# Wider first transfer of x, one copy of the norm weights and six narrower-operand warm-ups in a two-layer decoder kernel

## The reference

```python
def hybrid_layer(x, attn_norm, w_in, moba_out_norm, dil_out_norm, w_out, mlp_norm, w_up, w_down, cos, sin):
    h = rms_norm(x, attn_norm)            # x * rsqrt(mean(x*x) + eps) * gain
    qa, ka, va, qd, kd, vd = split(h @ w_in)              # 1024 -> 3072, 8 + 8 heads of 64
    out_a = rms_norm(causal_attention(rope(qa), rope(ka), va), moba_out_norm)
    out_d = rms_norm(dilated_attention(rope(qd), rope(kd), vd), dil_out_norm)
    x = x + concatenate([out_a, out_d]) @ w_out
    h = rms_norm(x, mlp_norm)
    return x + square(relu(h @ w_up)) @ w_down            # 1024 -> 4096 -> 1024
# two layers, then rms_norm(x, final_norm)
```

## Time and profile before

| | |
|---|---|
| median of 3 runs | 591.47 us (591.19 to 591.62) |
| the profiled execution | 591.49 us, span 589.8 us |
| TensorE busy | 581.0 us, 99% of the span |
| VectorE, ScalarE, GpSimd busy | 405.3, 314.2, 65.7 us |
| moved by DMA | 104.18 MB, mean 177 GB/s |

### The profile page before, as it was taken

One profiled execution on the slowest core, in us unless ns is written; L12 is line 12 of the kernel. 1 busy time (PEld: TensorE's weight loads), 2 busy tenths in 40 slices (PEclk: granted clock), 3 DMA queues, 4 the chain that ended last, 5 costly groups with the idle time before them and its releaser, 6 DMA issues.

```text
span 589.8 us, 9170 instructions
## 1 busy us (share of the span) xinstructions
PE 581.0 (99%) x3293; PEld 489.2 (83%) x3293; DVE 405.3 (69%) x652; ACT 314.2 (53%) x525; POOL 65.7 (11%) x67
## 2 busy tenths in 40 slices
PE   8999999999999999999999999999999999999995
PEld 6888877888888888888888888778888888888884
DVE  5897887597656656556379879768876656656634
ACT  5856867375445345344285765774645345345322
POOL 0242330210000000000005225112000000000001
PEclk9999999999999999999999999999999999999998
DMA  8955243258664564564264643442885564564301
GB/s 298 379 206 190 107 142 126 91 173 305 197 236 158 178 239 151 188 238 143 71 205 155 215 141 144 144 142 72 254 260 199 165 235 169 169 236 164 107 0 71
DMA packets 58859, 104.18 MB, mean 177 GB/s; under 512 B 1824, under 2 KB 35152, under 8 KB 58832
## 3 DMA queue, kind: packets, MB, share of 16 engines
q1 hardware_dynamic: 58256, 102.92, 51.8%
q10 hardware_dynamic: 576, 0.92, 0.5%
HBM read 102.79 MB, written 1.05 MB: 176 GB/s over the span
## 4 chain that ended last, share of the span: by engine, by line
PE 96%; DMA 1%; DVE 1%; ACT 1%; issue 0%; SPq 0%; POOLq 0%; POOL 0%; DVEq 0%
PE psum L1204 20%; PE psum L986 15%; PE psum L988 15%; PE psum L987 15%; PE psum L1207 10%; PE psum L1007 9%; PE psum L1012 4%; PE psum L1141 2%; PE psum L1160 2%; DMA raw<-in_w_in 1%; PE psum L1177 1%; PE psum L993 1%; PE psum L1180 1%; ACT xt L531 0%; DVE x L735 0%
## 5 line engine op out<-in xcount | busy, mean ns | idle before, releaser
L701 DVE TENSOR_TENSOR w_lo<-raw,w_hi 128x1024 fp32r<-128x1024 f32 x188 | 228.2, 1247 | 52.1 <-ACT w_hi L525 52.0
L525 ACT CAST w_hi<-raw 128x1024 fp32r<-128x1024 f32 x188 | 186.5, 1047 | 3.5 <-DMA raw<-in_w_in 2.8
L1204 PE MATMUL psum<-xt,w_hi 128*128 128x512 f32 x512 | 160.8, 395 | 0.0
L986 PE MATMUL psum<-w_hi,ot_hi 128*128 128x512 f32 x320 | 126.9, 397 | 0.0
L988 PE MATMUL psum<-w_hi,ot_lo 128*128 128x512 f32 x320 | 124.9, 390 | 0.0
L987 PE MATMUL psum<-w_lo,ot_hi 128*128 128x512 f32 x320 | 124.8, 390 | 0.0
L1207 PEld LDWEIGHTS psum<-xt,w_lo 128*128 128x128 f32 x512 | 96.2, 188 | 22.3
L1207 PE MATMUL psum<-xt,w_lo 128*128 128x256 f32 x512 | 100.7, 278 | 0.0
L1204 PEld LDWEIGHTS psum<-xt,w_hi 128*128 128x128 f32 x512 | 80.2, 189 | 2.3
L645 ACT COPY up_cross<-psum 128x512 f32<-128x512 f32 x32 | 18.8, 587 | 118.8 <-PE psum L1207 118.8
L879 DVE TENSOR_TENSOR up_cross<-psum,up_cross 128x512 f32<-128x512 f32 x32 | 22.1, 690 | 74.1 <-ACT up_cross L645 74.1
(11 more groups left out here) (98 smaller groups left out, 537.6 us busy)
## 6 DMA issues: line engine op xcount, KB each, us to landing
raw<-in_w_up SPq DMA_DIRECT2D x32, 1024.0 KB, 5.6
raw<-in_w_down SPq DMA_DIRECT2D x32, 1024.0 KB, 6.6
raw<-in_w_in SPq DMA_DIRECT2D x21, 1024.0 KB, 5.9
raw<-in_w_out SPq DMA_DIRECT2D x8, 1024.0 KB, 4.8
raw<-in_w_in SPq DMA_DIRECT2D x3, 512.0 KB, 8.2
raw<-in_w_in SPq DMA_DIRECT2D x4, 256.0 KB, 4.7
out<-x SPq DMA_DIRECT2D x3, 256.0 KB, 2.4
raw<-in_w_in ACTq DMA_DIRECT2D x2, 256.0 KB, 4.7
```

The source lines that it names most:

```text
L525: act.copy(dst, src).then_inc(hi_done, 1)
L701: dve.tensor_tensor(lo_t, src, hi_t, ALU.subtract).then_inc(split_done, 1)
L986: pe.matmul(out, s_hi, m_hi, start=first, stop=False)
L1204: pe.matmul(up_banks[b][:, f, :], w_hi[:, slot, cols[f]], xt[:, k, :, :].rearrange("p a b -> p (a b)"), start=k == 0, stop=False)
```

## The change

Four edits in one. SP's and ScalarE's first transfers of x carry columns 0 to 511 instead of 0 to 255, and SP's separate transfer of columns 256 to 511 is gone, with its semaphore. `gains` holds both layers' 48 columns and is written by one copy; `gains_all`, `keep_gains` and the copy at each layer's end are gone, and every use picks its layer's column. The ones of the warm-ups are 128 columns, repeated four times by the operand's access pattern, and there are six warm-ups at the start instead of seven.

```diff
-        gains_all = sb("gains_all", [n_gains + layer_gains])
-        gains = sb("gains", [layer_gains])
+        gains = sb("gains", [n_gains])
...
+        def layer_gain(l, n):
+            return gains[:, l * layer_gains + n:l * layer_gains + n + 1]
...
-            sp.dma_start(x[:, 0, 0:SEQ], x_v[:, 0, 0:SEQ]).then_inc(x_loaded[0], 16)
+            sp.dma_start(x[:, 0, 0:BANK], x_v[:, 0, 0:BANK]).then_inc(x_loaded[0], 16)
             sp.dma_start(gain_rows[:, :], gain_rows_d).then_inc(gains_loaded, 16)
-            sp.dma_start(x[:, :, SEQ:BANK], x_v[:, :, SEQ:BANK]).then_inc(x_loaded[1], 16)
...
-            act.dma_start(x[:, 1, 0:SEQ], x_v[:, 1, 0:SEQ]).then_inc(x_loaded[0], 16)
+            act.dma_start(x[:, 1, 0:BANK], x_v[:, 1, 0:BANK]).then_inc(x_loaded[0], 16)
...
                 act.wait_ge(turned, l * TRS + n + 1)
-                if n == TR_X:
-                    act.wait_ge(gains_done, l + 1)
-                act.activation(dst, tile, ACT.Copy, scale=gains[:, gain:gain + 1]).then_inc(turned_hi, 1)
+                act.activation(dst, tile, ACT.Copy, scale=layer_gain(l, gain)).then_inc(turned_hi, 1)
...
                     act.wait_ge(weights_used, UNITS_HELD)
+                    act.wait_ge(gains_kept, 1)
                     x_to_hi(l, 0)
...
-            dve.memset(squares[:, 1, 0:BANK], 1.0).then_inc(ones_set, 1)
+            dve.memset(squares[:, 1, 0:P], 1.0).then_inc(ones_set, 1)
 
             dve.wait_ge(gains_turned, 1)
-            dve.tensor_copy(gains[:, :], banks[7][:, 0:layer_gains]).then_inc(gains_done, 1)
-
-            def keep_gains():
-                dve.tensor_copy(gains_all[:, 0:n_gains], banks[7][:, 0:n_gains])
-                dve.tensor_copy(gains_all[:, n_gains:n_gains + layer_gains], banks[7][:, 0:layer_gains])\
-                    .then_inc(gains_kept, 1)
+            dve.tensor_copy(gains[:, :], banks[7][:, 0:n_gains]).then_inc(gains_kept, 1)
...
-                dve.wait_ge(gains_kept, 1)
-                dve.wait_ge(turned_lo, (l + 1) * TRS)
-                dve.tensor_copy(gains[:, :], gains_all[:, bass.ds((l + 1) * layer_gains, layer_gains)])\
-                    .then_inc(gains_done, 1)
...
-                    pe.matmul(banks[6][:, :], squares[:, 1, 0:P], squares[:, 1, 0:BANK], start=True, stop=True)
-
-            warm_up(7)
+                    pe.matmul(banks[6].rearrange("p (n q) -> p n q", q=P), squares[:, 1, 0:P],
+                              squares[:, 1:2, 0:P].broadcast_to([P, BANK // P, P]), start=True, stop=True)
+
+            warm_up(6)
...
                     if s == 1 and l == 0:
-                        pe.wait_ge(x_loaded[1], 16)
                         turn_x(x_banks, range(2, 3))
```

More of the change, by code:

```diff
@@ L191, in hybrid_kernel @@
         up_banks = [psum[:, 4:6, :], psum[:, 6:8, :]]
-        x_loaded = [sem(f"x_loaded{n}") for n in range(3)]
+        x_loaded = [sem(f"x_loaded{n}") for n in range(2)]
         masks_loaded = sem("masks_loaded")
@@ L225, in hybrid_kernel @@
         rope_scaled = sem("rope_scaled")
-        gains_done = sem("gains_done")
         rope_terms = sem("rope_terms")
@@ L327, in o_tile, with o_gain @@
             return o_bank[:, p % 2 * SEQ:(p % 2 + 1) * SEQ]
-        def o_gain(p):
-            column = p + (2 * KT + SET_PAIRS if p < SET_PAIRS else 2 * KT - SET_PAIRS)
-            return gains[:, column:column + 1]
+        def layer_gain(l, n):
+            return gains[:, l * layer_gains + n:l * layer_gains + n + 1]
+        def o_gain(l, p):
+            return layer_gain(l, p + (2 * KT + SET_PAIRS if p < SET_PAIRS else 2 * KT - SET_PAIRS))
         def visit(l, c):
@@ L370, in _ @@
                                      at(in_v[:, :, k:k + 1, cols], l)).then_inc((tile_loaded[2], raw_ready[0])[k - 2], 16)
-                    sp.dma_start(x[:, :, BANK:D_MODEL], x_v[:, :, BANK:D_MODEL]).then_inc(x_loaded[2], 16)
+                    sp.dma_start(x[:, :, BANK:D_MODEL], x_v[:, :, BANK:D_MODEL]).then_inc(x_loaded[1], 16)
                     for half in range(2):
@@ L539, in o_to_hi @@
             def o_to_hi(l, p):
-                act.activation(ot_hi[:, p, :], o_tile(p), ACT.Copy, scale=o_gain(p)).then_inc(o_hi_done, 1)
+                act.activation(ot_hi[:, p, :], o_tile(p), ACT.Copy, scale=o_gain(l, p)).then_inc(o_hi_done, 1)
             def square_sums(l, n):
@@ L705, in turned_to_lo @@
                 dve.wait_ge(turned_hi, l * TRS + left + 1)
-                dve.scalar_tensor_tensor(out=lo_t, in0=tile, scalar=gains[:, gain:gain + 1],
+                dve.scalar_tensor_tensor(out=lo_t, in0=tile, scalar=layer_gain(l, gain),
                                          in1=hi_t.bitcast(F32), op0=ALU.mult, op1=ALU.subtract)\
@@ L714, in o_to_lo @@
                 dve.wait_ge(o_hi_done, l * PAIRS + LAST_PAIR[p] + 1)
-                dve.scalar_tensor_tensor(out=ot_lo[:, p, :], in0=o_tile(p), scalar=o_gain(p),
+                dve.scalar_tensor_tensor(out=ot_lo[:, p, :], in0=o_tile(p), scalar=o_gain(l, p),
                                          in1=ot_hi[:, p, :].bitcast(F32), op0=ALU.mult, op1=ALU.subtract)\
@@ L798, in _ @@
                     dve.tensor_copy(tile_apart(w_hi, 0), as_loaded(raw[:, 0, 0:BANK])).then_inc(first_tile_hi, 1)
-                    dve.wait_ge(gains_done, 1)
+                    dve.wait_ge(gains_kept, 1)
                     for k in range(4):
@@ L802, in _ @@
                         x_lo(k)
-                        if k == 1:
-                            keep_gains()
                     tile_to_lo(4)
@@ L1260, in _ @@
                     if s == (3 if l == 0 else 2):
-                        pe.wait_ge(x_loaded[2], 16)
+                        pe.wait_ge(x_loaded[1], 16)
                         pe.wait_ge(x_updated, l * 4 + 4)
```

## The result

The changed kernel took 593.05 us (median of 16 runs, 592.05 to 593.98), the kernel before 591.41 us (median of 16, 590.94 to 591.71): 1.64 us more, a ratio of 1.0026, 95% interval [1.0019, 1.0033]. The forecast was 591.6, and the range ended at 592.8. The mechanism that decided is that of rival B, which had 0.14. The profiled execution took 592.73 us, span 591.0, 1.24 us more than that of before: one of the shorter of the 16. One execution of the kernel before, taken beside the experiments, was slowed as a whole (644.48 us at a granted clock of 0.85) and is counted nowhere.

A forecast was written before the change was run, and what follows sets the result against it. TensorE, busy 99% of the span, was taken to bound the kernel. 0.50 us late at the first k, less 0.09 and 0.24 filled, gave +0.17 us, so 591.65, rounded to 591.6; range 590.9 to 592.8.

The forecast's parts named there:

- rival B: At the start, the 0.7 us hole after the warm-ups keeps TensorE at 1.2 GHz: +1.4 us, 593.0; chance 0.14.
- What bounds it: Whole kernel: TensorE, busy 581.0 us, 99% of the span, sets the time; other engines have room.
- (4), the warm-ups: Start: smaller memset, six warm-ups from 1.47 to near 4.0, TensorE then idle 0.7 us, at no cost by itself.
- the profile's sign: What the profile would show under rival B: groups of four matmuls spaced 0.85 us behind 6.3.
- the transfers' term: Start: TensorE 0.50 us late at the first k, less the 0.09 and 0.24 it fills: +0.17 us.
- (1), the transfers: Start: wider transfers of x delay tile k = 0 from 5.2 to 6.1 and TensorE's second group by 0.50 us.
- The upper bound of 8.1: Latest landing of tile k = 1, cast by 8.75, making TensorE 0.25 us later still.
- The slack: TensorE before 17 us: holes of 0.09 and 0.24 us, 0.33 in all, that a late start can use up.
- (2), what comes back: Tiles k = 4 and 5: fewer packets and a shorter SP queue give back 0.06 to 0.77 us; landing not later.
- (3), the norm weights: Norm weights' copies: one 0.02 us longer, hidden; the dropped copies, 0.4 and 0.18 us, gain nothing.

The follow-up runs named there:

- b_warm3: The kernel before with three warm-ups instead of seven, its transfers and copies unchanged: 592.62 us, ratio 1.0017.
- a_warm7: The changed kernel with seven warm-ups at the start instead of six: 592.72 us, ratio 1.0020.
- b_wide: The kernel before with the wide first transfers of x alone, seven warm-ups and old copies kept: 591.92 us, ratio 1.0016.
- a_rowsfirst8: The changed kernel with eight warm-ups and SP issuing the norm weights before x: 592.16 us, ratio 1.0020.
- b_gains: The kernel before with the one copy of the norm weights alone, everything else as before: 591.41 us, ratio 1.0000.
- a_late6: The changed kernel with its six warm-ups begun later, at 2.11 instead of 1.30 us, behind an extra VectorE memset: 592.91 us, ratio 1.0026.
- a_warm8: The changed kernel with eight warm-ups at the start instead of six: 591.83 us, ratio 1.0010.
- a_xapart8: The changed kernel with the old narrow transfers of x and eight warm-ups instead of six: 591.36 us, ratio 1.0000.

## Why the prediction was wrong

**What bounds it.** Right. TensorE's stream sets the time: 1.30 us of lateness at the seventh k became 1.24 at the end.

**(4), the warm-ups.** This is the step that failed: "By itself that costs nothing, as transfers bound the start". The hole was forecast at 0.7 us and measured 1.08, as the memset took 0.17 instead of 0.25 us and started a little earlier (the warm-ups start at 1.30, not 1.47), and the norm weights landed at 5.0 and not 4.8 and were taken at 5.13. What stood in the place of "nothing" is the clock: 13 of 16 executions of the changed kernel are above 592.5, and with two warm-ups more, which lift it early in 10 of 11, 1.1 us of the median go.

Rival B had this mechanism, with the price (+1.1 us for a k at the lower level, 593.0 in sum) and the profile's sign (0.85 us between groups, which is what 7.79 and 8.64 show). It assumed that the first k and half of the second would be low, +1.4 us; it was just the first k in the profiled execution, 1.19 us of the second k's lateness. That B's sum of 593.0 meets the median of 593.05 is in part luck: its clock term was too large by about 0.2 to 0.3 us, and the transfers' term of 0.17 too small by 0.4. The transfers' miss alone would have left the time near 592.0, inside the range; the clock's took it out.

B's chance was the mistake. I held against it that the hole is short and transposes stand after it. b_warm3 and a_warm7 (a hole of 0.76 us, 7 of 11 late) show that neither protects. In the profiled executions the link is complete: the three with a rise past 9 us took 592.31, 592.71 and 592.73, and the ten others of the table, all with a rise by 7.2, took 591.07 to 591.92.

**(1), the transfers.** The direction was right, the size too small: +0.17 forecast, +0.56 measured in b_wide's lower group. Its terms: the transposes were priced at 0 to 0.1 late and were 0.41 late in b_wide, because the norm weights' landing was put at 4.7 to 4.9 and came at 5.1 there. The tile k = 0 was put at 6.1, and came near 5.7 in the changed kernel and 5.9 in b_wide, the lower bound or just above; the second group was 0.31 late in b_wide (7.19 against 6.88) where 0.50 was forecast. The tile k = 1 was put at 7.35 to 7.4 and called hidden; it came at 7.8, and it is the wait that TensorE meets. The upper bound of 8.1 for it was in the text, with its price of 0.25 us. So lateness moved to the tile behind the one that I watched. The slack was there: the changed kernel was 1.65 us late at the second k and 1.30 at the seventh, and the seventh k's weights were no longer waited for.

The direction holds beyond one pair of profiles. With the wide transfer the norm weights landed at 5.0 to 5.2, the tile k = 0 at 5.7 to 5.9 and the tile k = 1 at 7.5 to 7.9 (the six that keep the order of the issues, and a_rowsfirst8 for the tiles); with the old ones at 4.1 to 4.4, 4.9 to 5.6 and 6.6 to 7.4, in seven profiles each.

**(2), what comes back.** The direction was right: the tiles k = 4 and 5 landed at 10.9 instead of 11.8, 0.9 us earlier (forecast 0.06 to 0.77). Part of this is chance, for the seven profiles with the old transfers have this landing anywhere from 11.0 to 11.8, and the seven with the wide one from 10.9 to 11.2. SP issued these tiles 0.21 us earlier (3.42 instead of 3.63) and not at least 0.42, as the text had it for every later tile. Nothing waited for them any more, so all this only let the slack be used.

**(3), the norm weights.** Right: b_gains is at 1.0000.

**The clock's page.** By the Trainium skill (TensorE: Matmul & The Clock Gate, Part 4) transposes don't count as activity the way matmuls do. The runs show that they run at either level, 0.11 us apart at the upper and 0.21 at the lower; whether they count for the rise is not shown, since every kernel here has the same ones.

**What stays open.** How much work and how small a hole it takes, and what makes the executions of one kernel fall in two groups. The runs point to both influences (a_late6 against b_wide: 9 and 3 of 11 late, with one warm-up less, begun later, and the same hole; a_rowsfirst8 against a_warm8: 5 and 1 of 11, the same warm-ups with the hole grown), and to no rule. Both pairs ran on different chips, and the second difference is small for eleven executions. Part of it is not in the kernel at all: before and b_gains do the same work up to 5.3 us and rose near 5.4 and near 6.7. In the five profiled kernels without a hole, and the two whose hole opened only after the rise, the rise came 3.1 to 5.9 us after the start of the first warm-up (b_wide, a_xapart8). If a hole only matters in executions whose clock has not risen by then, two groups follow; no late execution was profiled beside an early one of the same kernel, so this is argued and not shown. One execution of each kernel was profiled, so the late groups of a_warm7, b_wide and a_rowsfirst8 are put to the clock by their distance, some 1.0 to 1.3 us between the medians of the groups, and not by a trace of their own.

## What to carry to other kernels

Warm-up matmuls are part of the schedule. Whoever shortens them, starts them sooner or delays what they cover should compare the end of the last one with the landing that follows, and look at the spacing of the first real matmuls, not at the granted clock alone. Here the clock rose late in a share of the executions only: the spread over ten runs tells of it before the median does, and one profile can show either case. And when bytes are moved ahead of a queue, price every tile behind them, up to the one that the bounding engine reaches with no lead.

## What the runs showed of the hardware that I had not expected

The lower level, once missed, lasted beyond the whole first k: the rise was near 9.3, 9.5 and 9.7 us in the three late profiles, by 7.2 in the others and never between. In the changed kernel TensorE had then been without a gap, by the profile, since 5.13. In a_xapart8, with no hole at all, it had worked 5.9 us before the rise, in b_wide 3.1. The profile's granted clock read 1.00 at both levels.

Issued as the second transfer of SP instead of the first, 0.45 us later, the same 256 KB of x landed at 5.8 instead of 4.9 (a_rowsfirst8 against a_warm8, 0.8 us by the single landings). What in the queues makes 0.8 of 0.45 wasn't taken apart.
